# Two-layer hybrid diffusion backbone on one core: latent attention scored with keys on the rows, low parts of the probabilities formed by VectorE from PSUM

## What is computed

```python
def block_softmax_attention(q, k, v):
...
    def one_block(qi):
        s = jnp.einsum('bqhd,bkhd->bhqk', qi, k, preferred_element_type=jnp.float32)
        p = jax.nn.softmax(s, axis=-1).astype(v.dtype)
        return jnp.einsum('bhqk,bkhd->bqhd', p, v)
```

## Time and profile before

| | us |
|---|---|
| median of 3 runs | 4261.07 |
| lowest, highest | 4256.55, 4267.57 |
| span of the profiled execution | 4261.7 |
| TensorE busy | 3720.1 (87%) |
| VectorE busy | 2267.7 (53%) |
| ScalarE busy | 1415.5 (33%) |
| GpSimd busy | 1306.3 (31%) |

### The profile page before, as it was taken

One profiled execution on the slowest core, in us unless ns is written; L12 is line 12 of the kernel. 1 busy time (PEld: TensorE's weight loads), 2 busy tenths in 40 slices (PEclk: granted clock), 3 DMA queues, 4 the chain that ended last, 5 costly groups with the idle time before them and its releaser, 6 DMA issues. The chain is left out here.

```text
span 4261.7 us, 54579 instructions
## 1 busy us (share of the span) xinstructions
PE 3720.1 (87%) x20116; PEld 3116.5 (73%) x20116; DVE 2267.7 (53%) x3970; ACT 1415.5 (33%) x2841; POOL 1306.3 (31%) x1182
## 2 busy tenths in 40 slices
PE   6997688877847899999999897698968788999998
PEld 4897577766625688888888697577847767888886
DVE  4853566656663344444444752576766625445454
ACT  3112466651111422222223312466741123222222
POOL 1211011123331155555554211011123313545454
PEclk8998799997868899999999898799978899999999
DMA  5530000012013111111110630000040122111111
GB/s 188 192 110 3 28 1 13 1 54 112 20 43 141 50 40 39 39 39 39 34 35 10 203 121 4 25 1 11 6 157 20 45 95 69 59 39 52 47 49 54
DMA packets 145678, 243.97 MB, mean 57 GB/s; under 512 B 9480, under 2 KB 113689, under 8 KB 141915
## 3 DMA queue, kind: packets, MB, share of 16 engines
q1 hardware_dynamic: 138108, 208.57, 14.8%
q0 software_dynamic: 7392, 33.03, 2.1%
HBM read 215.60 MB, written 25.99 MB: 57 GB/s over the span
## 5 line engine op out<-in xcount | busy, mean ns | idle before, releaser
L2242 POOL TENSOR_TENSOR x<-x,mlp_tmp 128x512 f32<-128x512 f32 x576 | 785.5, 1396 | 805.9 <-DVE mlp_tmp L2223 800.8
L2223 DVE TENSOR_TENSOR mlp_tmp<-psum,gate 128x512 f32<-128x512 f32 x576 | 391.8, 689 | 273.2 <-POOL x L2242 194.6
L143 PE MATMUL psum<-act_hi,w_hi 128*128 128x512 f32 (+1 forms) x1280 | 472.8, 369 | 12.6 <-DVE w_lo L2201 12.6
L144 PE MATMUL psum<-act_lo,w_hi 128*128 128x512 f32 (+1 forms) x1280 | 472.5, 369 | 0.0
L145 PE MATMUL psum<-act_hi,w_lo 128*128 128x512 f32 (+1 forms) x1280 | 472.4, 369 | 0.0
L143 PE MATMUL psum<-w_hi,hidden_hi 128*128 128x512 f32 x1152 | 449.9, 391 | 0.0
L144 PE MATMUL psum<-w_lo,hidden_hi 128*128 128x512 f32 x1152 | 448.4, 389 | 0.0
L145 PE MATMUL psum<-w_hi,hidden_lo 128*128 128x512 f32 x1152 | 448.2, 389 | 0.0
L2215 DVE TENSOR_TENSOR hidden_lo<-square,hidden_hi 128x512 fp32r<-128x512 f32 x160 | 102.4, 640 | 592.6 <-ACT hidden_hi L2187 592.6
L1378 DVE TENSOR_REDUCE att_max<-psum 128x1 f32<-128x512 f32 (+2 forms) x272 | 217.9, 801 | 183.5 <-PE psum L145 183.3
L2179 ACT ACTIVATE relu<-psum 128x512 f32<-128x512 f32 x160 | 88.9, 555 | 666.8 <-PE psum L145 666.8
(11 more groups left out here) (325 smaller groups left out, 8608.3 us busy)
## 6 DMA issues: line engine op xcount, KB each, us to landing
w_raw<-in_mlp_w SPq DMA_DIRECT2D x128, 512.0 KB, 3.8
side_w<-in_w_ada SPq DMA_DIRECT2D x40, 1024.0 KB, 6.5
hy_tab<-in_hy_tab POOLq DMA_DIRECT2D x24, 1024.0 KB, 13.6
w_raw<-in_w_in SPq DMA_DIRECT2D x32, 512.0 KB, 4.6
ada_w<-in_w_ada SPq DMA_DIRECT2D x8, 1024.0 KB, 11.5
x<-in_x SPq DMA_DIRECT2D x4, 2048.0 KB, 14.6
wo_raw<-in_w_out SPq DMA_DIRECT2D x16, 512.0 KB, 5.6
hy_scratch<-hy_out POOLq DMA_DIRECT2D x24, 256.0 KB, 3.1
```

Source lines behind the costliest of these rows:

```text
L143: pe.matmul(out, lhs[0], rhs[0], start=start, stop=False)
L144: pe.matmul(out, lhs[0], rhs[1], start=False, stop=False)
L2223: dve.tensor_tensor(tmp[:, j % 2, :], ps[:, 4 + j % 4, :], gate[:, int(t >= LAT_TILES), 512 * h:512 * h + 512], ALU.mult).then_inc(gated.s ...
L2242: pool.tensor_tensor(a, a, tmp[:, j % 2, :], ALU.add).then_inc(added.sem, 1)
```

## The change

The block of `phase_latent` is written anew. What it does now:

- Keys, values and queries are made with features on the partitions at once (`key_parts`, `query_parts`), head by head. Even heads keep their 64 plain rows at 0 to 63, odd heads at 64 to 127. The weights of the queries hold the rotated columns twice, the second time with halves swapped, so that the rotation is two products by VectorE (into `rope_a`, `rope_b`) and a sum by GpSimd.
- Scores come out turned: 128 keys on the partitions, 512 queries along the row. A block is one head with 512 latent queries (or, in layer 0, two heads with the 256 context queries); a slot is two key tiles of a block, five slots to a latent block and one to a context block.
- The maximum of a query is now needed before the scores and along the row. `rough_scores` makes scores of high parts only, with queries on the partitions, VectorE reduces them, and `max_row` spreads the maxima into a row of the queries' tile that faces a row of ones in the keys' tile. Thus the product itself subtracts the maximum. These are the tasks of the next block (`max_ctx`, four `max_lat`, `row`).
- ScalarE forms the exponential twice: rounded into `probs_hi`, and in full in PSUM over the scores. VectorE subtracts the one from the other (`probs_low`). `on_pool`, the set of slots whose low part GpSimd would form, is empty.
- The weighting takes three passes of 512 columns. Beside the high value columns stand 64 columns of ones, so the other 64 output rows hold the sums of the probabilities. ScalarE copies these to the value rows, VectorE inverts them there in two halves and multiplies.
- Side tasks (maxima of the next block, q of the next head, k and v of the next pair of heads) are dealt out over the half-slots of a block (`side`); they share banks 0 and 1. Everything for the first block is made in an opening, ahead of which GpSimd fills the constant rows (signal `lat_fixed`).

```diff
-            def turn_probs(n, k):
-                pe.wait_ge(exped.sem, exped[(n, len(keys(units[n])) - 1)])
-                at, c = turned_parts(n)[k]
-                i = t_index[(n, k)]
-                if i >= T_RING:
-                    pe.wait_ge(p_lo.sem, p_lo[t_parts[i - T_RING]])
-                bank = t_bank(n, k)
-                for m in range(c):
-                    last = pe.transpose(bank[:, m * P:(m + 1) * P], pe_[:, n % 2, (at + m) * P:(at + m + 1) * P],
-                                        kit.ident[:])
-                last.then_inc(p_turned.sem, 1)
...
-            def probs_lo(n, k):
-                at, c = turned_parts(n)[k]
-                dve.wait_ge(p_hi.sem, p_hi[(n, k)])
-                m = n // 2
-                dve.tensor_tensor(pl[m % 2][:, at:at + c, n % 2, :], t_bank(n, k).rearrange("p (a b) -> p a b", a=c),
-                                  ph[m % 2][:, at:at + c, n % 2, :].bitcast(F32), ALU.subtract).then_inc(p_lo.sem, 1)
...
+    for p in range(MLA_H // 2):
+        blocks += [Block([2 * p], 0, range(10)), Block([2 * p], 512, range(10))]
+        if context_too:
+            blocks += [Block([2 * p, 2 * p + 1], SEQ, range(8, 10))]
+        blocks += [Block([2 * p + 1], 0, range(10)), Block([2 * p + 1], 512, range(10))]
...
+    on_pool = set()
...
+    def max_tasks(b):
+        if blocks[b].context:
+            return [("max_ctx", b, 0), ("row", b, 0)]
+        return [("max_ctx", b, 0)] + [("max_lat", b, i) for i in range(4)] + [("row", b, 0)]
+
+    opening = [("v", 0, g) for g in range(3)] + [("kr", 0, g) for g in range(3)]
+    opening += [("k", 0, g) for g in range(3)] + [("q", 0, g) for g in groups] + max_tasks(0)
+    side = {}
+    for b, block in enumerate(blocks):
+        todo = []
+        if not block.context:
+            todo = [t for n in (b + 1, b + 2) if n < len(blocks) and (n == b + 1 or blocks[n - 1].context) for t in max_tasks(n)]
+            h, p = block.heads[0], block.heads[0] // 2
+            if block.col0 == 0 and h + 1 < MLA_H:
+                todo += [("q", h + 1, g) for g in groups]
+            at = 2 * (h % 2) + (block.col0 > 0)
+            if p + 1 < MLA_H // 2:
+                todo += [("k", p + 1, at)] if at < 3 else []
+                todo += [("v", p + 1, g) for g in {1: [0], 3: [1, 2]}.get(at, [])]
+        n = 2 * block.slots
+        for i in range(n):
+            side[(first[b] + i // 2, i % 2)] = todo[i * len(todo) // n:(i + 1) * len(todo) // n]
...
+            def rough_scores(t):
+
+                kind, b, i = t
+                if kind == "max_ctx":
+                    for h, cols, _ in blocks[b].parts():
+                        ready_wait(h, cols)
+                    for n, (h, c) in enumerate(blocks[b].query_tiles()):
+                        last = pe.matmul(psf[:, CTX * n:CTX * (n + 1)], query_h[h % 2][:, c:c + P],
+                                         keys_h[h // 2 % 2][h % 2][:, SEQ:TOK], start=True, stop=True)
+                else:
+                    h, c = blocks[b].query_tiles()[i]
+                    for n in range(2):
+                        last = pe.matmul(ps[:, n, :], query_h[h % 2][:, c:c + P],
+                                         keys_h[h // 2 % 2][h % 2][:, 512 * n:512 * (n + 1)], start=True, stop=True)
+                last.then_inc(made.sem, 1)
+
+            def max_row(t):
+                b = t[1]
+                pe.wait_ge(maxed.sem, maxed[b])
+                for i in range(4):
+                    last = pe.transpose(bank(t)[:, i * P:(i + 1) * P], mx[:, b % 2, i:i + 1].broadcast_to([P, P]), kit.ident[:])
+                last.then_inc(made.sem, 1)
...
+            def score(s):
+                b, j = slots[s]
+                if j == 0:
+                    pe.wait_ge(rowed.sem, rowed[b])
+                if s >= 2:
+                    if s - 2 in on_pool:
+                        pe.wait_ge(exped.sem, exped[s - 2])
+                    else:
+                        pe.wait_ge(lo_dve.sem, lo_dve[s - 2])
+                for i in range(2):
+                    k0 = blocks[b].key_tiles[2 * j + i] * P
+                    for h, cols, at in blocks[b].parts():
+                        last = three_pass(pe, ps[:, S0 + 2 * (s % 2) + i, at],
+                                          [a[h // 2 % 2][h % 2][:, k0:k0 + P] for a in (keys_h, keys_l)],
+                                          [a[h % 2][:, cols] for a in (query_h, query_l)], True, True)
+                last.then_inc(scored.sem, 1)
...
+                        one, low = weights_of(blocks[b].key_tiles[2 * j + i], h)
+                        out, begins, ends = ps[:, O0 + b % 2, at], j == 0 and i == 0, j == blocks[b].slots - 1 and i == 1
+                        pe.matmul(out, one, ph[s % 3][:, i, at], start=begins, stop=False)
+                        pe.matmul(out, low, ph[s % 3][:, i, at], start=False, stop=False)
+                        last = pe.matmul(out, one, pl[s % 3][:, i, at], start=False, stop=ends)
+                last.then_inc(weighed.sem, 1)
...
+            pe.wait_ge(fixed.sem, fixed["rows"])
+            pe.wait_ge(w_lo.sem, w_lo["ukv"])
...
+            for s in range(n_slots + 2):
+                if s < n_slots:
+                    score(s)
+                    for t in side[(s, 0)]:
+                        side_task(t)
+                if s >= 2:
+                    weigh(s - 2)
+                if s < n_slots:
+                    for t in side[(s, 1)]:
+                        side_task(t)
...
+            def exp(s):
+                act.wait_ge(scored.sem, scored[s])
+                if s >= 3:
+                    act.wait_ge(weighed.sem, weighed[s - 3])
+                scores = ps[:, S0 + 2 * (s % 2):S0 + 2 * (s % 2) + 2, :]
+                act.activation(ph[s % 3][:], scores, ACT.Exp, scale=SCALE)
...
+                    act.activation(scores, scores, ACT.Exp, scale=SCALE).then_inc(exped.sem, 1)
...
+                for e in range(2):
+                    link(pool, pool.memset(keys_h[b][e][SWAP[e], :].bitcast(F32), 1.0))
+                    link(pool, pool.memset(keys_l[b][e][SWAP[e], :].bitcast(F32), 0.0))
+            for e in range(2):
+                link(pool, pool.memset(query_h[e][SWAP[e], :].bitcast(F32), 0.0))
+                link(pool, pool.memset(query_l[e][SWAP[e], :].bitcast(F32), 0.0))
+            for b in range(2):
+                link(pool, pool.memset(v[b][:, :, V_ONES, :].bitcast(F32), 1.0))
+                link(pool, pool.memset(v[b][:, :, V_ZEROS, :].bitcast(F32), 0.0))
+            pool.memset(kr2[:, :, 32:64], 0.0).then_inc(fixed.sem, 1)
...
+            def side_task(t):
+                kind, h, g = t
+                if kind != "q":
+                    return
+                rows, cols = ROPE[h % 2], columns_of(g)
+                pool.wait_ge(freed.sem, freed[t])
+                clear = pool.memset(query_h[h % 2][SWAP[h % 2], cols].bitcast(F32), 0.0)
+                if g == 2:
+                    clear.then_inc(roped.sem, 1)
+                    pool.wait_ge(roped.sem, roped[t])
+                    return
+                link(pool, clear)
+                link(pool, pool.tensor_tensor(rot[rows, :], rot[rows, :], rot2[rows, :], ALU.add))
+                link(pool, pool.tensor_copy(query_h[h % 2][rows, cols], rot[rows, :]))
+                pool.tensor_tensor(query_l[h % 2][rows, cols], rot[rows, :], query_h[h % 2][rows, cols].bitcast(F32),
+                                   ALU.subtract).then_inc(roped.sem, 1)
+                pool.wait_ge(roped.sem, roped[t])
...
+                    e = n % 2
+                    if g < 2:
+                        turns = [q for q in tasks[:tasks.index(t)] if q[0] == "q" and q[2] < 2]
+                        if turns:
+                            dve.wait_ge(roped.sem, roped[turns[-1]])
+                        dve.tensor_tensor(rot[ROPE[e], :], bank(t)[ROPE[e], :], rope_t[ROPE[e], cols], ALU.mult)
+                        dve.tensor_tensor(rot2[ROPE[e], :], bank(t)[SWAP[e], :], rope_t[SWAP[e], cols], ALU.mult)
+                    for rows in [NOPE[e]] if g < 2 else WHOLE[e]:
+                        last = low(query_l[e][rows, cols], bank(t)[rows, 0:w], query_h[e][rows, cols])
+                last.then_inc(freed.sem, 1)
+
+            def probs_low(s):
+                dve.wait_ge(exped.sem, exped[s])
+                low(pl[s % 3][:], ps[:, S0 + 2 * (s % 2):S0 + 2 * (s % 2) + 2, :], ph[s % 3][:]).then_inc(lo_dve.sem, 1)
...
+            for s in range(n_slots + 3):
+                if s < n_slots:
...
+                        for t in side[(s, i)]:
+                            side_task(t)
+                    if s not in on_pool:
+                        probs_low(s)
+                if s - 2 in final:
+                    invert(final[s - 2], 0)
+                if s - 3 in final:
+                    invert(final[s - 3], 1)
+                    normalize(final[s - 3])
```

(23 more changed lines are left out.)

642 lines of the change are left out of this document (308 added, 334 removed).

## The result

The changed kernel took 4462.51 us (median of 4 runs, 4457.94 to 4463.5), the kernel before 4259.14 beside it: ratio 1.0469, 95% interval 1.0454 to 1.0484. Slower, as forecast, but by 203 us (by the medians, 4462.51 - 4259.14) where the forecast had 99 (4360 - 4261), and above the range of 4235 to 4435.

The account below looks back on a forecast made before the run. TensorE leads and how well it is fed decides, with VectorE's lag stalling it; phases of 492 and 441 us, 933 against 831, plus 102 on 4261.7 give 4364, taken as 4360 us; range 4235 to 4435.

Parts of the forecast that it names:

- Rivals 1 and 2: First: engines fed as well as before, 4285, chance 0.20; second: buffers of three absorb VectorE's lag, 4222, chance 0.16.
- TensorE idle until the fills end: Opening of each phase: TensorE and ScalarE wait for 17 constant fills on GpSimd, 18.8 us.
- VectorE's 352 and 319 us: VectorE's busy time in the two phases, forecast near 356 us in layer 0 and 324 in layer 1.
- the rotated product waiting 4 us: VectorE's rope products wait on GpSimd's subtraction for about 4 us, eight times in layer 0.
- the row waits 2 to 3 us: TensorE's row transposes wait on the maximum for 2 to 3 us in each block.
- Layer 1, "23.3": Layer 1, the first of two alternating blocks, 23.3 us, the other 25.7; the layer's phase 441 against 391.
- one low part comes between the two q: Layer 1 has nine tasks, not ten, so a low part separates the two query tasks: blocks of 23.3 and 25.7 us.
- The quiet ones: Layer 1 blocks without a query task, forecast at 25.7 us.
- Layer 0, 111 for a pair of heads: Layer 0, per pair of heads: 28.2 + 25.6 + 3 + 31.2 + 23.1 = 111 us; the phase 492 against 440.
- 3 (context block): Layer 0, the context block in each pair of heads, taken as 3 us of the 111.
- The openings, 55: Start of each phase: fills, keys, values, queries and rough maxima put the first score at about 55 us.
- Rival 3: The clock: gaps of 2 to 3 us twice a block, mean 0.85, plus 70 more, 4430; chance 0.12.

Follow-up runs that it names:

- e2: Changed kernel with two pairs of buffers for the rotated query halves, so VectorE's second product no longer waits for GpSimd's chain: 4407.24 us, ratio 1.0336.
- e4: Changed kernel without the division: 72 reciprocals left out, the product multiplies by the sum itself, so the output is wrong: 4317.58 us, ratio 1.0123.
- e6: Changed kernel with the low part of the second slot of each large block formed by GpSimd instead of VectorE: 4409.69 us, ratio 1.0338.
- e18: Changed kernel with eight idle matmuls ahead of the row of maxima, only in blocks without a query task: 4448.32 us, ratio 1.0430.

## Why the direction was right and the size wrong

The prediction's account of what decides, the feeding of TensorE and not its work, is borne out: 31 us for 77 of TensorE's, 147 for 125 of VectorE's. Rivals 1 and 2, in which TensorE waits less than in the layout, are refuted. Of its signs, TensorE idle until the fills end, VectorE's 352 and 319 us and the rotated product waiting 4 us came as listed; the row waits 2 to 3 us, but in 20 of 34 blocks. The first score, at 62.8 us and not 55, and the phases did not: they are 1031.6 us where it had 933. The 99 us (98.6), by block:

- **Layer 1, "23.3".** The step that failed most: "one low part comes between the two q", so GpSimd's chain was taken as hidden there. It isn't: `rope_a` waits for `qT_lo` 7 times, 21.7 us, in layer 1 too. The blocks with queries take 29.3; 7 x 6 = 42 us. Two buffers bring them to 24.9, so 4.4 of the 6 are this wait and what hangs on it. The quiet ones, forecast at 25.7, took 25.05 in the mean of the first six: 5 us less over eight.
- **Layer 0, 111 for a pair of heads.** It is 122: 32.2, 29.0, 35.3 and 26.0, by the copies from 695.93 to 818.50, for 28.2, 28.6, 31.2 and 23.1. Four times 11 is 44 us. Two terms are missing. The wait of the weighting behind context blocks, which "3 (context block)" left out, is 16.6 of it, and 12 when removed. And the layout took every matmul at 0.235 us. In the block of 32.2 us two series ran at the lower clock: from the row at 702.55 to 705.92 (granted 0.52), and behind the wait for the second query part from 717.03 to 722.89 (granted 0.51):

```profile
717.03 0.80 PE L143 MATMUL psum<-lat_hi,w_ukv_hi 128*128 128x512 f32 x1 [3.38 <-DVE qT_lo L1562]
717.62 0.63 PE L144 MATMUL psum<-lat_lo,w_ukv_hi 128*128 128x512 f32 x1
718.05 0.63 PE L145 MATMUL psum<-lat_hi,w_ukv_lo 128*128 128x512 f32 x1
```

By estimate, with 0.235 and 0.117 us for each, the two took 1.5 and 2.8 us longer than laid out, and the block is 4.0 longer. The first lies on the path: from the row to the first query part's low part the layout had 6.6 us, and it took 8.2 (702.55 to 710.79). For the second, and for the other blocks, that is an estimate and not shown; no run held the clock up in layer 0's query blocks alone. e2, e4 and e6 say that any relief of VectorE takes these blocks down.
- **The openings, 55.** The first score starts at 566.62, 62.8 us in; 7.8 late, and 7.6 in layer 1. The fills were right (17.9 us for 18.8). Behind them TensorE ran at 1.2 GHz (0.55 in the window), and the step that failed is again the durations at full clock. The changed kernel's rough maxima and first score:

```profile
554.32 1.22 PE L1337 MATMUL psum<-kT_hi,qT_hi 128*128 128x512 f32 x2 [1.32 <-DVE max_b L1574]
...
556.86 1.22 PE L1337 MATMUL psum<-kT_hi,qT_hi 128*128 128x512 f32 x2 [1.31 <-DVE max_a L1580]
...
566.62 0.77 PE L143 MATMUL psum<-qT_hi,kT_hi 128*128 128x512 f32 x1 [0.77 <-ACT qT_hi L1449]
```

The maxima come 2.54 us apart where 1.95 was taken (five of them, 3 us); v, keys and the first query part were done 41.3 us in, for 36.6.

Sum: 42 - 5 + 44 + 16 = 97 of 99.

**Rival 3** foresaw 4430 from the clock. Its mean, 0.85, agrees with the phases (0.84, 0.86) by luck: these hold the openings, at 0.55, and over the blocks, for which it was worked out, the clock is 0.89 and 0.91. Its mechanism is shown by the 0.43 us behind a wait. Its price is not settled. A matmul taken away anywhere gave less than half of its time (31 for 77), but behind the row of a quiet block of layer 1 holding the clock up gave 1.6 us, and the 17 us of e18 are for a rise of 2 to 3 hundredths, of the 9 to 11 that the blocks lack. The rule of the Trainium skill (TensorE: Matmul & The Clock Gate, HAM oscillation) agrees with this trace on the fall, which came after waits like the 3.20 us above. The divide's repeat count in the Trainium skill (VectorE: DVE Perf Modes, First, the fixed hardware budget) gave an estimate of 2.13 us for the reciprocal; it took 1.743.

## What to carry to other kernels

When two engines are each busy 70 to 85% and wait for each other in order, neither share bounds the kernel: time the block, take a known amount from each engine in turn, and see which gives more than it lost. A helper chain on a third engine must be laid out for every variant of the task order, with its full latency, and a double buffer for its input is the cheapest cure. When the clock falls behind a stall, remove the stall's cause first: the second buffers gave 57 us and brought the clock of the steady stretch from 0.91 to 0.94, idle matmuls gave 17. And in a layout by hand, what stands behind a wait of 2 to 3 us is not to be taken at full clock.

## What the runs showed of the hardware

- A group of 32 partitions takes GpSimd as long as 128 (1.27 and 1.29 us for 512 columns of a sum; 0.602 for a rounding copy into `qT_hi` and 0.615 for the six of 128 partitions into `lat_hi` in the same run), and VectorE's reciprocal costs the same on 64 as on 128 (1.743 and 1.753): columns count.
- Raising 64 x 512 values to a power on GpSimd took 82.2 us, 160 ns a column, against 6.8 ns a column for VectorE's reciprocal.
- Behind waits of 2.3 to 3.4 us the granted clock was 0.51 to 0.56 over the next 3 to 6 us, and matmuls of 512 columns started 0.43 us apart instead of 0.235. Eight matmuls that compute nothing, ahead of the wait, kept the clock at 0.97 over a stretch where it was 0.91, and bought 17 us.
